# Latent projections of an encoder layer: f32 products replaced by three f16 products each

## The reference

```python
q = (rms_norm(cq, q_a_norm) @ w_uq).reshape(B, L, N_HEADS, QK_HEAD)        # 256 -> 8 x 96
kv = (rms_norm(ckv, kv_a_norm) @ w_ukv).reshape(B, L, N_HEADS, QK_NOPE + V_HEAD)  # 128 -> 8 x 128
k_nope, v = kv[..., :QK_NOPE], kv[..., QK_NOPE:]
q = rms_norm(q, q_norm)   # k likewise, with the shared rotary columns
```

## Time and profile before

| | us |
|---|---|
| median of 3 timed runs | 2719.81 |
| lowest, highest | 2709.26, 2720.89 |
| the profiled execution | 2716.53 |
| its span | 2714.7 |
| first loop of `project` | 0 to 145 |
| second loop and its tail | 145 to 545 |

### The profile page before, as it was taken

One profiled execution on the slowest core, in us unless ns is written; L12 is line 12 of the kernel. 1 busy time (PEld: TensorE's weight loads), 2 busy tenths in 40 slices (PEclk: granted clock), 3 DMA queues, 4 the chain that ended last, 5 costly groups with the idle time before them and its releaser, 6 DMA issues. The chain is left out here.

```text
span 2714.7 us, 51042 instructions
## 1 busy us (share of the span) xinstructions
PE 2479.3 (91%) x20059; PEld 1387.5 (51%) x20059; DVE 1905.9 (70%) x2642; ACT 1647.3 (61%) x2326; POOL 1144.4 (42%) x1032
## 2 busy tenths in 40 slices
PE   6899999879999999998898989799954899999997
PEld 4455555426666666663332233354533566666664
DVE  5446767647777777777898989566646577777773
ACT  6634455338888888887655855343434666676651
POOL 1224444226666666667303900244312355444531
PEclk9999999959999999998999989899965899999999
DMA  7413345344411212026796888655543899999972
GB/s 189 129 35 122 115 140 172 117 85 153 114 40 42 47 40 48 25 52 206 256 329 215 292 282 307 198 157 172 156 147 106 263 265 283 264 261 260 275 190 51
DMA packets 392346, 448.05 MB, mean 165 GB/s; under 512 B 205454, under 2 KB 270478, under 8 KB 389840
## 3 DMA queue, kind: packets, MB, share of 16 engines
q1 hardware_dynamic: 367632, 372.73, 45.0%
q0 software_dynamic: 12288, 38.05, 5.9%
q10 hardware_dynamic: 12224, 34.48, 3.7%
HBM read 270.67 MB, written 137.91 MB: 151 GB/s over the span
## 5 line engine op out<-in xcount | busy, mean ns | idle before, releaser
L1254 POOL TENSOR_TENSOR at_p<-at_pf,at_p 128x512 f16<-128x512 f32 x325 | 378.6, 1173 | 263.3 <-ACT at_p L1389 262.9
L1530 DVE TENSOR_REDUCE at_mxs<-at_pM 128x1 f32<-128x512 f32 x512 | 343.9, 688 | 104.6 <-PE at_pM L1420 102.7
L1388 ACT ACTIVATE at_pf<-at_pS,at_scale 128x1024 f32<-128x1024 f32 x260 | 289.8, 1115 | 110.2 <-PE at_pS L1451 105.6
L1389 ACT ACTIVATE at_p<-at_pS,at_scale 128x1024 f16<-128x1024 f32 x260 | 287.8, 1107 | 0.0
L1476 PE MATMUL at_pO<-at_vv,at_p 128*128 128x65 f16 x2080 | 227.0, 194 | 3.1 <-POOL at_p L1254 3.1
L1477 PE MATMUL at_pO<-at_vv,at_p 128*128 128x64 f16 x2080 | 226.4, 195 | 0.0
L1479 PE MATMUL at_pO<-at_vv,at_p 128*128 128x65 f16 x2080 | 225.8, 193 | 0.0
L1420 PE MATMUL at_pM<-at_kT,at_qT 96*128 96x512 f16 x512 | 200.1, 393 | 15.7 <-DMA at_qT<-s_QK 12.5
L1477 PEld LDWEIGHTS at_pO<-at_vv,at_p 128*128 128x128 f16 x2080 | 195.2, 98 | 37.5 <-issue 1.1
L1476 PEld LDWEIGHTS at_pO<-at_vv,at_p 128*128 128x128 f16 x2080 | 195.3, 97 | 35.0 <-issue 3.3
L1449 PE MATMUL at_pS<-at_qT,at_kT 97*128 97x512 f16 (+1 forms) x528 | 202.0, 383 | 3.4 <-DMA at_qT<-at_nmx 2.2
(11 more groups left out here) (423 smaller groups left out, 6237.5 us busy)
## 6 DMA issues: line engine op xcount, KB each, us to landing
sp_rows<-s_F SPq DMA_DIRECT2D x76, 512.0 KB, 5.6
s_F<-fs_a SPq DMA_DIRECT2D x72, 512.0 KB, 3.2
mo_raw<-in_w_gate SPq DMA_DIRECT2D x32, 1024.0 KB
mo_raw<-in_w_up SPq DMA_DIRECT2D x32, 1024.0 KB
mo_down<-in_w_down SPq DMA_DIRECT2D x32, 1024.0 KB, 4.9
s_QK<-pj_R ACTq DMA_DIRECT2D x18, 1024.0 KB, 3.9
s_G<-sp_gg SPq DMA_DIRECT2D x72, 256.0 KB, 4.2
sp_tab<-tab_spec SPq DMA_DIRECT2D x76, 224.0 KB, 4.0
```

Of the source, the lines that this page charges most:

```text
L1254: eng.tensor_tensor(p2[r][:, half, :], pf[:, r, half, :], p1[r][:, half, :], ALU.subtract).then_inc(own_done if own(g, half) else others_d ...
L1388: act.activation(pf[:, r, :, :], pS[g % 2][:, :, :], ACT.Exp, scale=scale[:, 0:1])
L1389: act.activation(p1[r][:, :, :], pS[g % 2][:, :, :], ACT.Exp, scale=scale[:, 0:1]).then_inc(p_made, 1)
L1530: dve.tensor_reduce(mxs[:, j // NC, j % NC:j % NC + 1], pM[j % 2][:, :], AX.X, ALU.max).then_inc(pM_free, 1)
```

## The change

Each f32 product of the query, key and value steps becomes three f16 products that add up in the same PSUM bank: high latent by high weight, high by low, low by high.

- The weights are loaded as f32 into the end of the tile `c` (the rows of tiles 11 to 17, free until ACT copies those latents) and are no longer in tiles of their own. SP issues the two loads a little later in its list, behind a wait for the four splits of the latents' columns of `w_in`, which lay there.
- They are sized (ACT squares them in pass 6, PE adds over partitions in pass 8, ACT moves the result, POOL takes the power in pass 9), and in pass 9 ACT makes the high f16 part of each and DVE the low part. ACT's copy of `c` for tile 11 waits for both low parts, and so does PE's second loop.
- To have them early, `scale_weights` goes from pass 4 to pass 2 on DVE, `size_gains` from 5 to 3, `bound_values` from 8 to 4, `scale_values` from 12 to 5, and the matching square, sum and power on ACT, PE and POOL from 5 to 3, 6 to 4 and 11 to 6.
- In the second loop ACT's copy of the transposed latents writes f16 with a factor of 1024 (`cH`), and DVE gets a new step, `split_c(m)`, in the slots with n % 3 = 0, behind all its other work of the slot: it takes the transposed latents from PSUM, subtracts `cH` and writes `cL`. The query products and the next tile's transposes wait for it.
- ACT's moves of q, k and v multiply by `l_back`.

```diff
@@ sync @@
-            sp.dma_start(wkv[:, :], io["w_ukv"][0]).then_inc(lt_in, 16)
-            sp.dma_start(wq[:, :, :], io["w_uq"][0].rearrange("(k p) f -> p k f", p=P)).then_inc(lt_in, 16)
...
+            sp.wait_ge(cL_made, C_PARTS)
+            sp.dma_start(wkv[:, :], io["w_ukv"][0]).then_inc(l_in, 16)
+            sp.dma_start(wq[:, :, :], io["w_uq"][0].rearrange("(k p) f -> p k f", p=P)).then_inc(l_in, 16)
@@ gpsimd @@
+            def scale_latent():
+                pool.wait_ge(l_sized, 1)
+                pool.tensor_tensor(l_size[:, :], l_size[:, :], tiny2[:, :], ALU.add).then_inc(l_sized, 1)
+                pool.wait_ge(l_sized, 2)
+                pool.tensor_tensor(l_scale[:, :], l_size[:, :], mhalf[:, 0:2], ALU.pow).then_inc(l_scaled, 1)
...
-                if t == NT // 2 + 2:
+                if t == 6:
                     pool.wait_ge(v_sized, 1)
...
+                if t == 9:
+                    scale_latent()
@@ scalar @@
+                if t == RAW_FROM:
+                    act.wait_ge(l_low, 2)
...
+                if t == 6:
+                    act.wait_ge(scaled, 6)
+                    act.activation(wqH[:, :, :], wq[:, :, :], ACT.Square, scale=1 / MOST, accum_out=l_sum[:, 0:1]).then_inc(l_squared, 1)
+                    act.activation(wkvH[:, :], wkv[:, :], ACT.Square, scale=1 / MOST, accum_out=l_sum[:, 1:2]).then_inc(l_squared, 1)
+                if t == 8:
+                    act.wait_ge(l_summed, 1)
+                    act.activation(l_size[:, :], pL, ACT.Copy).then_inc(l_sized, 1)
+                if t == 9:
+                    act.wait_ge(l_scaled, 1)
...
+                    act.activation(wqH[:, :, :], wq[:, :, :], ACT.Copy, scale=l_scale[:, 0:1]).then_inc(l_high, 1)
+                    act.activation(wkvH[:, :], wkv[:, :], ACT.Copy, scale=l_scale[:, 1:2]).then_inc(l_high, 1)
...
-                act.activation(cT[m % 2][:, :, :], pT.rearrange("p (k t) -> p k t", k=3), ACT.Copy).then_inc(cT_ready, 1)
+                act.activation(cH[m % 2][:, :, :], pT.rearrange("p (k t) -> p k t", k=3), ACT.Copy, scale=C_SCALE).then_inc(high_c, 1)
@@ tensor @@
+                if t == 8:
+                    pe.wait_ge(l_squared, 2)
+                    pe.wait_ge(f_chain, F_STEPS + len(FCH))
+                    pe.matmul(pL, ones[:, :], l_sum[:, :], start=True, stop=True).then_inc(l_summed, 1)
...
             def make_q(m):
-                pe.wait_ge(cT_ready, m + 1)
+                pe.wait_ge(low_c, m + 1)
...
-                        last = pe.matmul(pQ[:, n0:n1], cT[m % 2][:, k, :], wq[:, k, n0:n1], start=(k == 0), stop=(k == 1))
+                        for x, w in ((cH, wqH), (cH, wqL), (cL, wqH)):
+                            last = pe.matmul(pQ[:, n0:n1], x[m % 2][:, k, :], w[:, k, n0:n1],
+                                             start=(k == 0 and x is cH and w is wqH), stop=(k == 1 and x is cL))
@@ vector @@
+            def split_latent():
+                dve.wait_ge(l_high, 1)
+                dve.scalar_tensor_tensor(wqL[:, :, :], wq[:, :, :], l_scale[:, 0:1], wqH[:, :, :], ALU.mult, ALU.subtract
+                                         ).then_inc(l_low, 1)
...
+            def split_c(m):
+                dve.wait_ge(high_c, m + 1)
+                if m >= 2:
+                    dve.wait_ge(k_made, m - 1)
+                dve.scalar_tensor_tensor(cL[m % 2][:, :, :], pT.rearrange("p (k t) -> p k t", k=3), C_SCALE, cH[m % 2][:, :, :],
+                                         ALU.mult, ALU.subtract).then_inc(low_c, 1)
...
+                if n % 3 == 0 and m < NT:
+                    split_c(m)
```

More of the change, by code:

```diff
@@ L272 @@
 MOST = 2.0 ** 15
+C_SCALE = 1024.0
+assert C_SCALE * QL ** 0.5 < MOST
 def project(nc, io):
@@ L315, in project @@
         eye = sb("eye", [P, P])
-        wq, wkv = sb("wq", [P, 2, NH * QH]), sb("wkv", [P, NH * (ND + VH)])
+        wqH, wqL = (sb(f"wq{n}", [P, 2, NH * QH], F16) for n in "HL")
+        wkvH, wkvL = (sb(f"wkv{n}", [P, NH * (ND + VH)], F16) for n in "HL")
+        l_sum, l_size, l_scale, l_all, l_back, tiny2 = (sb("l_" + n, [P, 2]) for n in ("sum", "size", "scale", "all", "back", "tiny"))
         rope = sb("rope", [P, NT, 2 * RD])
@@ L329, in project @@
         w1, w2 = cn[0:2 * FEAT, 0, 0:P], cn[:, 0, P:2 * P]
-        cT = [sb(f"cT{b}", [P, 3, P]) for b in range(2)]
+        cH, cL = ([sb(f"c{n}{b}", [P, 3, P], F16) for b in range(2)] for n in "HL")
         ss, sse, rh = sb("ss", [P, H2]), sb("sse", [P, H2]), sb("rh", [P, H2])
@@ L691, in move_q @@
                     act.wait_ge(low_made, m - 1)
-                act.activation(qk[m % 2][:, 0:NH, :], pQ[:, 0:NH * QH].rearrange("p (h d) -> p h d", h=NH), ACT.Copy
-                               ).then_inc(q_moved, 1)
+                if m == 0:
+                    act.wait_ge(l_backed, 1)
+                act.activation(qk[m % 2][:, 0:NH, :], pQ[:, 0:NH * QH].rearrange("p (h d) -> p h d", h=NH), ACT.Copy,
+                               scale=l_back[:, 0:1]).then_inc(q_moved, 1)
             def move_k(m):
@@ L699, in move_k @@
                 of_k = pK.rearrange("p (h d) -> p h d", h=NH)
-                act.activation(qk[m % 2][:, NH:, 0:ND], of_k[:, :, 0:ND], ACT.Copy)
-                act.activation(v[m % 2], of_k[:, :, ND:], ACT.Copy).then_inc(k_moved, 1)
+                act.activation(qk[m % 2][:, NH:, 0:ND], of_k[:, :, 0:ND], ACT.Copy, scale=l_back[:, 1:2])
+                act.activation(v[m % 2], of_k[:, :, ND:], ACT.Copy, scale=l_back[:, 1:2]).then_inc(k_moved, 1)
             def square_heads(m):
@@ L859, in make_k @@
                 for n0 in (0, 512):
-                    last = pe.matmul(pK[:, n0:n0 + 512], cT[m % 2][:, 2, :], wkv[:, n0:n0 + 512], start=True, stop=True)
+                    for x, w in ((cH, wkvH), (cH, wkvL), (cL, wkvH)):
+                        last = pe.matmul(pK[:, n0:n0 + 512], x[m % 2][:, 2, :], w[:, n0:n0 + 512],
+                                         start=(x is cH and w is wkvH), stop=(x is cL))
                 last.then_inc(k_made, 1)
@@ L921, in scale_weights @@
             def scale_weights():
-                dve.wait_ge(lt_in, 16 * 7)
+                dve.wait_ge(lt_in, 16 * 5)
+                dve.wait_ge(l_in, 32)
                 for k in range(2):
```

41 lines of the change are left out of this document (29 added, 12 removed).

## The result

| | before | after |
|---|---|---|
| median of 20 runs each, us | 2710.82 (2702.44 to 2723.59) | 2721.49 (2707.56 to 2727.97) |
| ratio to before, with its 95% interval | | 1.0029 (1.0018 to 1.0041) |
| profiled execution, span, us | 2714.7 | 2725.9 |
| mean granted TensorE clock of the timed runs (before: 35 runs) | 0.952 | 0.949 |

The change made the kernel slower, by 0.29% or 7.9 us (4.9 to 11.1); the two medians happen to lie 10.7 us apart, and the text goes by the ratio, since the interval belongs to it. The forecast was a gain of 0.9 us. The size is inside the 0.5% that was given as the bound, but the sign is the other one. The page of the profile answers the earlier trace rows: the span is 11 us longer although PE is busy for 11 us less.

What follows compares the result with a forecast made beforehand. A ring of ACT, POOL and DVE paces the first loop and PE bounds the second. First loop +6.3 and second -7.2 sum to -0.9 us: 2715.6 profiled, 2719 beside the 2719.8 median; range 2704 to 2733.

Steps and rivals of the forecast that it cites:

- The saving on PE: Second loop: query step falls from 2.59 to 1.94 us, key and value step from 1.72 to 1.30; 19.3 us in all.
- The second loop, -7.2: Second loop: waits for DVE's new split leave 0.4 us a tile of the possible 1.07, so -7.2 us for 18 tiles.
- The held root: First loop, pass 9: POOL sizes the weights ahead of tile 10's root; about 6.3 us of idle PE, +5.5 us.
- Its loads are no new cost: First loop: SyncE reaches the moved weight loads near 26.6 us, the splits they wait for end at 25.2; no added time.
- the +1.0 for the scaling: First loop: weight scaling moved to DVE's pass 2 makes tile 5 late by 1.9 us, partly recovered at tile 6; +1.0 us.
- The squares, +2.9: First loop, pass 6: ACT squares both weights on the ring with no cover; +2.9 us.
- Copies and splits at no cost: First loop, pass 9: f16 copies on ACT and splits on DVE fall into existing waits; nothing, or 3 us without that cover.
- What follows this stage is untouched, and starts about 1 us earlier: Stages behind the changed one: no change of their own, only a start about 1 us earlier.
- the first (PE keeps its saving): Second loop: DVE catches up at every slot, -19.3 us kept, 2703 to 2707 us; chance 0.14 of over 0.5% faster.
- the second (DVE's wait as the loop's clock): Second loop: DVE's wait for the high copy delays all 11 chunk boundaries, 2 us each costing 22 us; chance 0.12.
- the third (a first loop at no cost but the squares): First loop: size returns in time, only 2.9 us stay; net -4 to -7, 2713 to 2716 us; chance 0.2.
- the fourth: PE products: f16 products 256 wide are held by their weight load, so the change fails its aim; chance under 0.02.

Runs made afterwards that it cites:

- experiment 6: Changed kernel with the two latent weight loads issued after the rows of x tiles 3 and 4; ratio to before 1.0003, second loop from 150.4 us.
- the other orders mended: Changed kernel with POOL's root order, latents' turn, SyncE's store and weight loads all reordered; ratio to before 0.9944, second loop from 140.5 us.
- the early turn: Changed kernel with the latents transposed, copied and split one slot earlier, DVE's split ahead of the convolutions; ratio to before 0.9968, second loop 390.0 us.
- before, store late: Kernel before with SyncE's store of the filter's hidden rows moved to the first loop's last step; ratio to before 0.9959.
- root first: Changed kernel with POOL sizing the latent weights after the root of tile 10 instead of before it; ratio to before 1.0001.

## Why the prediction was wrong in its sign

1. **The saving on PE: right.** 1.95 and 1.30 us a step, as forecast.
2. **The second loop, -7.2: right to the tenth, for the reason given; the last tenth is luck.** The split takes 0.556 us (0.55 taken). PE's waits stand where they were named: 1.37 us in slot 39 and 0.92 in slots 9 and 24 (1.4 forecast), 0.29 in slots 15, 30 and 45 (0.3 to 0.5), 1.3 at tile 12 (1.0 to 1.5). DVE's wait in slot 33 is 2.0 us and not 2.8, and PE's waits for the split sum to 6.0 us, not 10 to 12. But without the split or with its place mended the loop is 9 to 10 us shorter. 2.1 us of the 19.3 are lost elsewhere.
3. **The held root: right in mechanism, short in size.** 5.8 us of idle PE against "about 6.3". POOL's add and power took 1.0 us (89.75 to 90.72), inside the 0.8 to 1.8 given. Tile 10 loses 6.6 us by it, where +5.5 stood in the sum. Net of the chunk wait it was priced at 5.5 - 3.1 = 2.4 us, and is worth 5.1: the wait of 3.12 us was credited to it in full, while with the root mended a wait of 3.71 comes back and the start is still 5.1 us earlier.
4. **"Its loads are no new cost": the step that failed.** It asked whether the loads are issued later, and not what they stand in front of. Both go out at 25.06 and 25.43, 0.5 us ahead of the rows of x tile 3. These rows are issued 1.6 us earlier than before (25.91 for 27.52) and squared 1.3 us later (33.38 for 32.05). Before, then after:

```profile
32.05 1.06 ACT L570 ACTIVATE pj_R<-pj_R 128x1024 bf16<-128x1024 f32 x1 [2.35 <-DMA pj_R<-in_x_prompt]
```
```profile
25.43 0.44 SPq L461 DMA_DIRECT2D pj_c<-in_w_uq  x1
25.91 0.46 SPq L260 DMA_DIRECT2D pj_R<-in_x_prompt  x1
```

At tile 6, where the prediction closed its account, the changed kernel is 3.6 us late and not 1.0. With the loads behind the rows (experiment 6) it is 1.1 us late there, so the +1.0 for the scaling is borne out and the loads cost 2.5 us. At the second loop's start they cost 4.1.
5. **The squares, +2.9: about right** (2.5 us on ACT, 2.6 at tile 9). The size's other steps, counted at nothing beside the held root, bring the sizing without that root to 5.1 us.
6. **Copies and splits at no cost: right, in this order only.** The cover is SyncE's order, and the prediction took it for the load's own time. It named what they cost if it is gone (3 us). No run prices them alone without the cover; the whole preparation is 17.0 us then, and 140.5 - 135.5 = 5.0 us with the other orders mended.
7. **"What follows this stage is untouched, and starts about 1 us earlier": the other failure.** The code is untouched, the time is not: 5 of the 7.9 us. The trace of before can't show this; the range had clock scatter in it, the sum had nothing.

The first loop's sum was +6.3 us, and +9.9 was measured. By tiles 8, 9 and 10: loads and scaling +3.1 for 1.0, squares +2.6 for 2.9, root +6.6 for 5.5, and 2.4 us came back for 3.1. So the loads are the largest miss, with the root's size and the credit behind it. With these 3.6 us and the 5 of term 7 the sum of -0.9 is about +7.7, and 7.9 was measured. That the time lies inside the range of 2704 to 2733 is no merit of the sum: the range was wide enough for either sign.

Of the rivals, the first (PE keeps its saving) is what the early turn brings, by an edit; the second (DVE's wait as the loop's clock) did not happen, since the loop kept its 7.2 us; the third (a first loop at no cost but the squares) fell with the gap at tile 10; the fourth fell with the spacing of 0.11 us at 256 columns.

## What to carry over

A step that is moved in front of others in a queue is to be priced by what it stands in front of, at each queue: in single traces, whose starts can be some 3 us apart, POOL's held root cost 5.1 us, the weight loads ahead of x tile 3 4.1, DVE's split behind a convolution and not ahead of it 10, SyncE's store 9.1 in the kernel before. A wait that the profile gives to a DMA is not a slow DMA until its issue has been looked up: that for chunk 8 was a late issue, that for chunk 7 a slow load. And where a stage gains or loses some 3 us, the rest of the kernel must be compared too, over several traces of each version, since one pair can differ there by more.

## What the runs showed of the hardware

The granted clock fell to half (0.50, the 1.2 GHz level) 3 to 6 us after the last of the stage's products (`L824` before), in the tail, where PE was waiting. In the kernel before these products end at 529.5, and the stretches up to the fall and from there to the attention's first product are (PE was busy for 1.53 of 4.20 us, then for 3.56 of 18.10):

```profile
529.50:533.70 4.20, 1.53 (x12) 0.88 (x9) 3.57 (x4) 1.65 (x5) 0.00 (x0) 1.00 0.48 143
533.70:551.80 18.10, 3.56 (x14) 2.50 (x15) 1.19 (x3) 2.65 (x5) 0.76 (x4) 0.50 0.72 164
```

In all 17 traces the low level lasted into the attention stage, and it came again for that stage's last 7 to 11 us; together it took 35 to 62 us of the stage. The stage's length, up to the next stage's first product, follows this time closely: 683.7 us with 35.2 us at the low level (before, store late), 693.8 with 62.3 (root first), a slope of 0.34 us per us (correlation 0.99). The traces fall into two groups, eight with 35 to 37 us and nine with 55 to 62, and both groups have kernels with f32 and with f16 products. The two traces of before lie in the second, at 57.1 and 58.0 us. So a single pair of traces can be 7 to 10 us apart for this alone.
